# Neighbourhood attention: where a projection rests between its chunks, the order of the transfers, and the last head's output

## The chip, the core and the metric

One core of a Trainium2 chip runs the whole program in one launch. TensorE (PE) multiplies; VectorE (DVE), ScalarE (ACT) and GpSimd (POOL) work on its results; SyncE (SP) issues nearly all DMA transfers. Each engine runs its own list in order and waits on semaphores. The metric is the time of one execution in microseconds. It is 2857.19 us before the change, the median of three runs.

## The reference

The program is a trunk of two layers in fp32: a gated short convolution with its FFN, then neighbourhood attention with its FFN, and a final norm. Only the attention, its two projections and the passage into its output projection are touched.

```python
# layer 1 of a two-layer trunk; layer 0 is a gated short convolution, each layer ends in a SwiGLU FFN
def neighbourhood_attention(hl, hc, w_qkv, rpb, w_o, want_ctx):
    ...
    qkv = hl @ w_qkv                                   # 1024 latent tokens, 16 heads of 64
    kv_c = hc @ w_qkv[:, D:]                           # 256 context tokens: keys and values only
    ...
    def row_block(r):                                  # a row of 64 tokens of the 16 x 64 grid
        ...
        s_win = einsum('bhqd,bhrqcd->bhqrc', q_r, k_win) * scale + bias     # 8 x 16 window
        s_ctx = einsum('bhqd,bkhd->bhqk', q_r, k_ctx) * scale
        s = jnp.concatenate([s_win, s_ctx], axis=-1)
        p = jax.nn.softmax(s, axis=-1)
        ...
        return p_win @ v_win + p_ctx @ v_ctx
    ...
    yl = o.transpose(1, 0, 3, 2, 4).reshape(B, S, D) @ w_o
xl = xl + g1 * yl
```

## The kernel before

**Precision.** Every matrix product runs as three products of a high and a low part (`hi*hi`, `lo*hi`, `hi*lo`). So each intermediate is copied out of a PSUM bank twice: ScalarE writes the high part, and VectorE or GpSimd subtracts it for the low part.

**Pairs, units, groups.** The 16 heads make 8 pairs. For each pair the 1024 queries of each head are cut in four units of two blocks of 128, so a pair has 8 units, 0 to 3 for the first head and 4 to 7 for the second. A block scores against itself, its neighbours and the 256 context tokens: 640 keys, 512 at the ends. The turned probabilities of a unit are handled in three groups (`GROUPS`), so a pair has 24 slots: slot 3u + g is group g of unit u.

**TensorE's order.** In `attention` each slot does at most four things: `scores` of a block two units ahead (in groups 0 and 1 only), `fill` (a chunk of the Q or K projection of the NEXT pair), `turn` (transposes, two groups ahead), and `values` (the product with V). `values` of a unit's first group waits for `sum_done`, since all units share one PSUM bank. `QK_CHUNKS` says how many of a tile's 24 matmuls each slot gets. There are five tiles (`QK_TILES`): 0 is the context keys (256 columns), 1 and 3 are keys, 2 and 4 queries (512 columns); tiles 1 to 4 are those of the next pair, tile 0 that of the pair after. All use one bank, so behind each tile there is an empty slot, in which `QK_DRAINED` lets ScalarE (`qk_high`) and VectorE (`qk_low`) copy it out.

**ScalarE's order.** In a unit it takes `exponentials` of the next unit's first block, `pt_high` of group 0, the second `exponentials`, `pt_high` of group 1, `half` (the copy of half of the former unit's values), `pt_high` of group 2, and `out_high` (the high copy of the former unit's output). A drain stands behind its group's `pt_high`. `PANEL_AT` adds the high part of a weight panel at the end of two units. VectorE sums the halves (`head_sum`, which sets `sum_done`), GpSimd normalises the probabilities and makes low parts.

**SyncE's order.** Q and K go through DRAM: `store_qk` writes a tile, and `load_head0`, `load_late_keys0`, `load_late_queries0` and `load_head1` bring them back per head. A load waits until the store in front has landed, and all that is behind it on SP waits too. Unit outputs go from `o_st_hi` and `o_st_lo` to `o_dram` (`store_o`), and `load_o` brings them to `o_hi` and `o_lo` for the output projection, which multiplies eight blocks; block 7 is the last pair's.

**The ends.** Before the loop the first pair's five tiles are made in whole (`FIRST_BANKS`), among the last two tiles of V. The last pair has no projection to fill with.

## Time and profile before

| | |
|---|---|
| runs | 2856.08, 2857.23, 2857.19 us; median 2857.19 |
| profiled execution | 2855.52 us, its span 2853.7 us |
| PE busy | 2750.7 us, 96% |
| DVE, POOL, ACT busy | 1936.4, 1092.6, 952.6 us |
| attention | about 1588 to 2033 us of the span |
| output projection | about 2033 to 2137 us |

A row of a timeline has the start, the duration, the engine, the line and the operation with its tiles (out<-in); in square brackets stands how long the engine had been idle, and what released it. TensorE's records overlap, since a matmul's duration reaches to its last result: the pace is the difference between two starts. In rows of stretches PEclk is the granted clock of TensorE, 1.00 at 2.4 GHz and 0.50 at 1.2 GHz.

### The profile page before, as it was taken

Reading aid. Unit: us, or ns where it says so; the run is one execution under the profiler, and the core shown is the slowest. Engines: PE = TensorE matmul, PEld = TensorE weight load, DVE = VectorE, ACT = ScalarE, POOL = GpSimd, SP = SyncE. Lnnn points to the kernel's source line nnn. Section 1 sums busy time; section 2 is a strip of 40 time slices with the busy share of each in tenths; the row PEclk is TensorE's granted clock in tenths of the full one; section 3 lists DMA queues with packets and bytes.
Section 4 is the critical chain, followed back from the end, with each engine's and each line's share of the span. In section 5 each row is a group of like instructions: output and inputs, shape, how many; then the busy total and the mean of one; then the engine's idle time right before and its main releaser. Section 6 shows DMA issues by size and latency. Waiting matters only on the chain.

```text
span 2853.7 us, 42028 instructions
## 1 busy us (share of the span) xinstructions
PE 2750.7 (96%) x14290; PEld 2282.9 (80%) x14290; DVE 1936.4 (68%) x2826; ACT 952.6 (33%) x1678; POOL 1092.6 (38%) x792
## 2 busy tenths in 40 slices
PE   6999999999999999999999999999899999999998
PEld 3888888677788888889988788888777778888885
DVE  4677676778777777754765355656557877777777
ACT  4211111522222222244631466666423222222223
POOL 1212111125665565510011355445312566556552
PEclk9999999999999999999999999999999999999999
DMA  6421221032111111178567556555821011111111
GB/s 246 126 67 60 94 70 45 1 108 67 65 48 51 59 44 51 52 249 275 170 194 193 168 180 198 160 179 177 286 97 44 30 59 45 51 59 44 51 59 67
DMA packets 190148, 305.97 MB, mean 107 GB/s; under 512 B 58976, under 2 KB 123744, under 8 KB 190048
## 3 DMA queue, kind: packets, MB, share of 16 engines
q1 hardware_dynamic: 190048, 304.64, 33.1%
q8 instruction: 63, 1.03, 0.2%
q14 instruction: 37, 0.30, 0.0%
HBM read 255.28 MB, written 52.82 MB: 108 GB/s over the span
## 4 chain that ended last, share of the span: by engine, by line
PE 83%; DVE 5%; ACT 3%; DMA 3%; issue 3%; SPq 2%; POOL 1%; ACTq 0%; DVEq 0%; POOLq 0%
PE psum L1294 22%; PE psum L1146 20%; PE psum L1105 17%; PE psum L1479 6%; PE psum L1432 3%; PE psum L1344 3%; PE psum L1132 2%; PE psum L1538 2%; PE psum L1509 2%; PE psum L1355 1%; PE psum L1523 1%; DMA raw<-ffn_panels 1%; ACT probs L2025 1%; DVE w_lo L2387 1%; DVE residual L2250 1%
## 5 line engine op out<-in xcount | busy, mean ns | idle before, releaser
L2250 DVE SCALAR_TENSOR_TENSOR residual<-psum,modulation,residual 128x512 f32<-128x512 f32 x896 | 639.4, 729 | 376.2 <-PE psum L1146 372.8
L2791 POOL TENSOR_TENSOR w_lo<-raw,w_hi 128x1024 fp32r<-128x1024 f32 x118 | 295.5, 2511 | 909.0 <-ACT w_hi L1666 904.2
L1146 PE MATMUL psum<-prod_hi,w_hi 128*128 128x512 f32 x896 | 350.0, 391 | 11.3 <-DVE residual L2250 6.4
L1146 PE MATMUL psum<-prod_hi,w_lo 128*128 128x512 f32 x896 | 343.0, 383 | 0.0
L1146 PE MATMUL psum<-prod_lo,w_hi 128*128 128x512 f32 x896 | 343.0, 383 | 0.0
L2824 POOL TENSOR_TENSOR w_lo<-raw,w_hi 128x512 fp32r<-128x512 f32 x175 | 259.2, 1481 | 209.7 <-ACT w_hi L1829 209.7
L1666 ACT ACTIVATE w_hi<-raw 128x1024 fp32r<-128x1024 f32 x186 | 194.0, 1057 | 418.5 <-PE psum L1105 202.4
L1294 PE MATMUL psum<-act_hi,w_hi 128*128 128x512 f32 x700 | 273.6, 391 | 6.0 <-POOL w_lo L2824 5.9
L1294 PE MATMUL psum<-act_hi,w_lo 128*128 128x512 f32 x700 | 272.7, 390 | 0.0
L1294 PE MATMUL psum<-act_lo,w_hi 128*128 128x512 f32 x700 | 272.4, 389 | 0.0
L1146 PEld LDWEIGHTS psum<-prod_hi,w_hi 128*128 128x128 f32 x896 | 168.1, 188 | 70.8 <-DVE residual L2250 30.3
L1829 ACT ACTIVATE w_hi<-raw 128x512 fp32r<-128x512 f32 x175 | 109.4, 626 | 344.8 <-PE psum L1294 343.6
L1105 PE MATMUL psum<-act_hi,w_hi 128*128 128x512 f32 x728 | 194.8, 367 | 4.7 <-POOL w_lo L2809 3.0
L1146 PEld LDWEIGHTS psum<-prod_hi,w_lo 128*128 128x128 f32 x896 | 168.3, 188 | 34.0
L1105 PE MATMUL psum<-act_lo,w_hi 128*128 128x512 f32 x728 | 194.1, 366 | 0.0
L1105 PE MATMUL psum<-act_hi,w_lo 128*128 128x512 f32 x728 | 193.9, 366 | 0.0
L1146 PEld LDWEIGHTS psum<-prod_lo,w_hi 128*128 128x128 f32 x896 | 168.4, 188 | 28.3
L2462 DVE TENSOR_TENSOR part<-psum,part 128x512 f32<-128x512 f32 x245 | 167.3, 683 | 33.7 <-ACT part L1884 31.2
L2674 DVE TENSOR_TENSOR pt_lo<-psum,pt_hi 128x512 fp32r<-128x512 f32 (+1 forms) x192 | 111.0, 579 | 99.0 <-ACT pt_hi L2031 98.5
L1294 PEld LDWEIGHTS psum<-act_hi,w_hi 128*128 128x128 f32 x700 | 131.4, 188 | 36.0 <-POOL w_lo L2824 8.6
L1105 PEld LDWEIGHTS psum<-act_hi,w_hi 128*128 128x128 f32 x728 | 130.6, 188 | 32.5 <-ACT gate L1810 3.8
L1294 PEld LDWEIGHTS psum<-act_hi,w_lo 128*128 128x128 f32 x700 | 131.4, 188 | 28.0
(262 smaller groups left out, 6161.5 us busy)
## 6 DMA issues: line engine op xcount, KB each, us to landing
raw<-ffn_panels SPq DMA_DIRECT2D x198, 512.0 KB, 3.3
raw<-conv_panels SPq DMA_DIRECT2D x32, 512.0 KB, 5.4
rest_in<-mod_rest SPq DMA_DIRECT2D x40, 384.0 KB, 4.6
more_row<-mod_panels SPq DMA_DIRECT2D x48, 256.0 KB, 2.7
v_st<-v_dram SPq DMA_DIRECT2D x32, 320.0 KB, 4.9
mod_in<-mod_rest SPq DMA_DIRECT2D x24, 384.0 KB, 6.0
mod_early<-mod_panels SPq DMA_DIRECT2D x16, 512.0 KB, 15.2
raw<-qk_panels SPq DMA_DIRECT2D x16, 512.0 KB, 5.7
```

The costliest lines, as they stand in the source:

```text
L1105: mm = pe.matmul(psum[:, bank + b, 0:tn], w[:, s, kb, :], acts[h][:, kb, t0:t0 + tn], start=(kb == 0 and n == 0), stop=(kb == KB - 1 and n ...
L1146: mm = pe.matmul(psum[:, 6 + r % 2 if bank is None else bank, 0:tn], w[:, s, ob, :], h[:, t0:t0 + tn], start=(n == 0), stop=(n == 2))
L1294: mm = pe.matmul(psum[:, SEVEN_BANKS[n], :], w[:, where // 2, (where % 2) * KQ + q, :], moving[b][q], start=first, stop=last)
L1344: mm = pe.matmul(psum[:, bank, 0:TC], w[:, s, kb, :], h[:, kb, CTX], start=(kb == 0 and n == 0), stop=(kb == KB - 1 and n == 2))
L1479: mm = pe.matmul(psum[:, bank, 0:tn], w[:, s, kb, :], h[:, kb, t0:t0 + tn], start=(r == 0), stop=(r == QK_MATMULS - 1))
L1666: act.activation(panel(w_hi, s), raw[:, s], ACT.Copy).then_inc(hi_done[s], 1)
L1829: act.activation(quad(w_hi, where), source, ACT.Copy).then_inc(block_hi, 1)
L2250: dve.scalar_tensor_tensor(out=residual[:, ob, t0:t0 + tn], in0=psum[:, 6 + r % 2 if bank is None else bank, 0:tn], scalar=modulation[:, g ...
L2462: dve.tensor_tensor(part[:, out, :], psum[:, SEVEN_BANKS[n], :], part[:, other, :], ALU.add).then_inc(partial_dve, 1)
L2674: dve.tensor_tensor(pt_lo[:, at:at + n], psum[:, 4 + (group0[u] + g) % 2, 0:n], pt_hi[:, at:at + n], ALU.subtract).then_inc(pt_lo_done, 1)
L2791: pool.tensor_tensor(panel(w_lo, s), raw[:, s], panel(w_hi, s), ALU.subtract).then_inc(lo_done[s], 1)
L2824: pool.tensor_tensor(quad(w_lo, where), source, quad(w_hi, where), ALU.subtract).then_inc(block_lo, 1)
```

## The change

It does five things.

- `QK_CHUNKS`, `QK_DRAINED`: tile 1 takes slots 0 to 4 (5, 5, 5, 5, 4 matmuls), tile 2 slots 6 and 7 (12, 12), tile 3 slots 9 to 13, tile 4 slots 15 to 19, the narrow tile slots 21 and 22 (12, 12). The empty slots are 5, 8, 14, 20 and 23, where they were 4, 8, 13, 17 and 23. `PANEL_AT` moves one panel from unit 4 to unit 5.
- The first pair: all five tiles are made and drained first, the last two tiles of V after them, then the scores of two units. ScalarE's table load for the exponentials comes before the V copies.
- SP: in the first pair the late keys and queries go ahead of the V transfers; `load_head1` is split in keys and queries; in the loop the transfers stand in another order.
- The last pair's outputs are written to `o_hi` and `o_lo` in place, by rows of the head and not of two staging halves; the last stores and loads fall away. `head_sum` there waits for one unit later (`others` is 0).
- `last_pair` on TensorE waits for the low copies, not for a load.

TensorE, end of unit 6 in the loop (slots 19 or 20 and on; L1523 `turn`, L1538 `values`, L1509 `scores`, L1479 or L1478 the projection). Before, from the last matmul of the chunk in slot 20:

```order
L1479 MATMUL psum<-act_hi,w_lo 128x256
...
L1523 MATMUL psum<-ident,probs 128x128 [waits pt_lo_done]
L1538 MATMUL psum<-pt_hi,v_st 128x256 [waits pt_lo_done]
L1538 MATMUL psum<-pt_lo,v_st 128x256
L1538 MATMUL psum<-pt_hi,v_st 128x256
L1538 MATMUL psum<-pt_lo,v_st 128x256
...
L1509 MATMUL psum<-k_hi,q_st 128x256 [waits s_done]
L1509 MATMUL psum<-k_lo,q_st 128x256
L1509 MATMUL psum<-k_hi,q_st 128x384
L1509 MATMUL psum<-k_lo,q_st 128x384
```

After, from the last `values` of slot 19:

```order
L1538 MATMUL psum<-pt_lo,v_st 128x128
...
L1523 MATMUL psum<-ident,probs 128x128 [waits pt_lo_done]
L1538 MATMUL psum<-pt_hi,v_st 128x256 [waits pt_lo_done]
L1538 MATMUL psum<-pt_lo,v_st 128x256
L1538 MATMUL psum<-pt_hi,v_st 128x256
L1538 MATMUL psum<-pt_lo,v_st 128x256
...
L1509 MATMUL psum<-k_hi,q_st 128x256 [waits s_done]
L1509 MATMUL psum<-k_lo,q_st 128x256
L1509 MATMUL psum<-k_hi,q_st 128x384
L1509 MATMUL psum<-k_lo,q_st 128x384
...
L1478 MATMUL psum<-act_hi,w_hi 128x256 [waits lo_done1]
```

The chunk between the two `values` is gone: slot 20 is empty, and slot 21 starts a tile.

ScalarE, same place (`stage_hi` is a drain, `o_st_hi` the output copy, `w_hi` the panel, `probs` exponentials, `pt_hi` turned probabilities). Before:

```order
L2037 ACTIVATE o_half<-psum 64x256 [waits sum_done,pv_ready]
...
L2031 ACTIVATE pt_hi<-psum 128x512 [waits pt_ready]
L2044 ACTIVATE o_st_hi<-o_sum 64x256 [waits o_out1,sum_done]
L1666 ACTIVATE w_hi<-raw 128x1024 [waits raw_in0]
...
L2025 ACTIVATE probs,stats<-neg_s,stats 128x512 [waits s_done]
...
L2031 ACTIVATE pt_hi<-psum 128x512 [waits pt_ready]
...
L2025 ACTIVATE probs,stats<-neg_s,stats 128x640 [waits s_done]
```

After:

```order
L2035 ACTIVATE o_half<-psum 64x256 [waits sum_done,pv_ready]
...
L2029 ACTIVATE pt_hi<-psum 128x512 [waits pt_ready]
...
L2006 ACTIVATE stage_hi<-psum 128x512 [waits qk_out]
L2043 ACTIVATE o_st_hi<-o_sum 64x256 [waits o_out1,sum_done]
L1663 ACTIVATE w_hi<-raw 128x1024 [waits raw_in0]
...
L2023 ACTIVATE probs,stats<-neg_s,stats 128x512 [waits s_done]
...
L2029 ACTIVATE pt_hi<-psum 128x512 [waits pt_ready]
...
L2023 ACTIVATE probs,stats<-neg_s,stats 128x640 [waits s_done]
```

The drain of 512 columns now stands in front of the output copy, the panel and the next unit's exponentials.

SP, the first pair (`v_dram` stores of V, `k_dram` and `q_dram` stores of tiles 3 and 4). Before:

```order
L776 DMA v_dram<-stage_v_lo 128x8x64
L776 DMA v_dram<-late_v_hi 128x8x64 [waits v_lo_done,v_hi_done]
L776 DMA v_dram<-stage_v_lo 128x8x64
L799 DMA k_dram<-stage_hi 128x512 [waits qk_lo_done]
L799 DMA k_dram<-stage_lo 128x512
L813 DMA k_hi<-k_dram 64x512 [waits qk_out]
L813 DMA k_hi<-k_dram 64x512
L813 DMA k_lo<-k_dram 64x512 x2
L841 DMA v_st<-v_dram 128x640 x2
L799 DMA q_dram<-stage_hi 128x512 [waits qk_lo_done,v_out1,v_out0]
L799 DMA q_dram<-stage_lo 128x512
L807 DMA q_st<-q_dram 64x512 [waits qk_out]
```

After:

```order
L812 DMA k_dram<-stage_hi 128x512 [waits qk_lo_done]
L812 DMA k_dram<-stage_lo 128x512
L826 DMA k_hi<-k_dram 64x512 [waits qk_out]
L826 DMA k_hi<-k_dram 64x512
L826 DMA k_lo<-k_dram 64x512 x2
L812 DMA q_dram<-stage_hi 128x512 [waits qk_lo_done]
L812 DMA q_dram<-stage_lo 128x512
L820 DMA q_st<-q_dram 64x512 [waits qk_out]
L820 DMA q_st<-q_dram 64x512
L857 DMA v_st<-v_dram 128x640 [waits rest_summed]
L857 DMA v_st<-v_dram 128x640
L789 DMA v_dram<-late_v_hi 128x8x64 [waits v_lo_done,v_hi_done]
```

The stores of V went from in front of both tiles to behind them.

```diff
+        def staged_rows(i, u):
+            h0 = DH * (u // 4 if isinstance(i, int) and i == PAIRS - 1 else u % 2)
+            return slice(h0, h0 + DH)
+        def staged(i, u):
+            rows = staged_rows(i, u)
+            if isinstance(i, int) and i == PAIRS - 1:
+                q0 = 2 * P * (u % 4)
+                return rows, o_hi[rows, i, q0:q0 + 2 * P], o_lo[rows, i, q0:q0 + 2 * P]
+            return rows, o_st_hi[rows, :].bitcast(F32R), o_st_lo[rows, :].bitcast(F32R)
         def value_bank(i, u):
...
         QK_MATMULS = 3 * KB
-        FIRST_BANKS = (2, 3, 4, 5, PV_BANK)
+        FIRST_BANKS = (2, 3, 4, 5, 1)
...
-        QK_CHUNKS = {**chunks(1, 1, 0, (6, 6, 6, 6)), **chunks(1, 2, 5, (8, 8, 8)), **chunks(1, 3, 9, (6, 6, 6, 6)),
-                     **chunks(1, 4, 14, (8, 8, 8)), **chunks(2, 0, 18, (5, 5, 5, 5, 4))}
-        QK_DRAINED = {4: (1, 1), 8: (1, 2), 13: (1, 3), 17: (1, 4), 23: (2, 0)}
-        PANEL_AT = {4: 1, 6: 0}
+        QK_CHUNKS = {**chunks(1, 1, 0, (5, 5, 5, 5, 4)), **chunks(1, 2, 6, (12, 12)), **chunks(1, 3, 9, (5, 5, 5, 5, 4)),
+                     **chunks(1, 4, 15, (5, 5, 5, 5, 4)), **chunks(2, 0, 21, (12, 12))}
+        QK_DRAINED = {5: (1, 1), 8: (1, 2), 14: (1, 3), 20: (1, 4), 23: (2, 0)}
+        PANEL_AT = {5: 1, 6: 0}
...
-            def load_head1(i):
-                sp.wait_ge(qk_out, 32 * (NQK * i + Q_LAST + 1))
+            def load_keys1(i):
+                sp.wait_ge(qk_out, 32 * (NQK * i + K_LAST + 1))
                 at_least(sp, s_ready, 16 * i)
                 load_keys(i, 1, 0, T, head_in[1])
+            def load_queries1(i):
+                sp.wait_ge(qk_out, 32 * (NQK * i + Q_LAST + 1))
                 load_queries(i, 1, 0, TL, head_in[1])
...
             load_head0(0)
+            store_qk(0, K_LAST)
+            load_late_keys0(0)
+            store_qk(0, Q_LAST)
+            load_late_queries0(0)
             sp.wait_ge(rest_summed, MORE_GROUPS + V_LAST)
+            load_v(0, 0)
             store_v(V_LATE)
             store_v(V_LATE + 1)
-            store_qk(0, K_LAST)
-            load_late_keys0(0)
-            load_v(0, 0)
             for n in range(V_STAGES):
                 sp.wait_ge(v_out[n], 32 * len(V_ORDER) // V_STAGES)
-            store_qk(0, Q_LAST)
-            load_late_queries0(0)
-            load_head1(0)
+            load_keys1(0)
+            load_queries1(0)
             store_qk(1, 0)
...
                 first = isinstance(i, int) and i == 0
-                if panels:
-                    load_qk_panel(i + 2, 0)
-                    load_qk_panel(i + 2, 1)
-                elif heads:
-                    for s in range(2):
-                        load_panel("wo", s, 0, wo_panels[s])
-                load_v(i, 1)
+                if heads:
+                    load_bias(i + 1, 0)
                 if not first:
                     store_o(i - 1, UNITS - 1)
+                load_v(i, 1)
                 if not heads:
-                    load_o(2)
-                if heads:
-                    load_bias(i + 1, 0)
-                store_o(i, 0)
...
-                if not heads:
+                    for pair in range(2, PAIRS - 1):
+                        load_o(pair)
                     sp.wait_ge(s_ready, 2 * UNITS * PAIRS)
...
                         load_panel("wo", s, 0, wo_panels[s])
+                    return
+                store_o(i, 0)
+                store_qk(i + 1, 1)
+                for s in range(2):
+                    if panels:
+                        load_qk_panel(i + 2, s)
+                    else:
+                        load_panel("wo", s, 0, wo_panels[s])
+                store_o(i, 1)
+                store_qk(i + 1, 2)
+                load_head0(i + 1)
+                store_o(i, 2)
+                load_bias(i + 1, 1)
+                store_o(i, 3)
+                store_qk(i + 1, K_LAST)
+                load_v(i + 1, 0)
+                load_late_keys0(i + 1)
+                store_o(i, 4)
+                load_keys1(i + 1)
+                store_o(i, 5)
+                store_qk(i + 1, Q_LAST)
+                load_late_queries0(i + 1)
                 store_o(i, 6)
...
                     store_qk(i + 2, 0)
-                elif heads:
+                load_queries1(i + 1)
+                if not panels:
+                    load_o(0)
                     load_o(1)
...
-            for n in range(K_LAST):
+            for n in range(NQK):
                 if FIRST_BANKS[n] == V_REST_BANK:
                     pe.wait_ge(rest_ready, 2 * MORE_GROUPS + V_LAST)
+                if n == Q_LAST:
+                    pe.wait_ge(v_lo_done, V_LATE + 2)
                 qk_matmuls(0, n, FIRST_BANKS[n], 0, QK_MATMULS)
...
             v_tile(V_LATE + 1)
-            qk_matmuls(0, K_LAST, FIRST_BANKS[K_LAST], 0, QK_MATMULS)
...
                         values(i, u, g)
-            pe.wait_ge(v_lo_done, len(V_ORDER) + 4)
-            pe.wait_ge(qk_lo_done, K_LAST)
+            pe.wait_ge(qk_lo_done, NQK)
             for ab in range(2):
                 scores(0, 0, ab)
-            qk_matmuls(0, Q_LAST, FIRST_BANKS[Q_LAST], 0, QK_MATMULS)
-            scores(0, 1, 0)
+            for ab in range(2):
+                scores(0, 1, ab)
+            pe.wait_ge(v_lo_done, len(V_ORDER) + 4)
             qk_matmuls(1, 0, QK_BANK, 0, QK_MATMULS)
             pe.wait_ge(attn_consts, 5)
-            pe.wait_ge(qk_lo_done, K_LAST + 1)
             turn(0, 0, 0)
             turn(0, 0, 1)
-            scores(0, 1, 1)
-            pe.wait_ge(qk_lo_done, NQK)
             attention(0, 2)
...
                 if kb == PAIRS - 2:
-                    pe.wait_ge(o_last_in, 32)
+                    pe.wait_ge(o_lo_done, UNITS * PAIRS)
...
-                h0 = DH * (u % 2)
+                rows, high, _ = staged(i, u)
                 act.wait_ge(sum_done, UNITS * i + u + 1)
-                at_least(act, o_out[u % 2], 16 * UNITS * i + 32 * (u // 2))
-                act.activation(o_st_hi[h0:h0 + DH, :].bitcast(F32R), o_sum[h0:h0 + DH, :],
-                               ACT.Copy).then_inc(o_hi_done, 1)
+                if not (isinstance(i, int) and i == PAIRS - 1):
+                    at_least(act, o_out[u % 2], 16 * UNITS * i + 32 * (u // 2))
+                act.activation(high, o_sum[rows, :], ACT.Copy).then_inc(o_hi_done, 1)
...
                 n = UNITS * i + u
-                h0 = DH * (u % 2)
+                others = 0 if isinstance(i, int) and i == PAIRS - 1 else 1
                 dve.wait_ge(half_done, n + 1)
-                at_least(dve, o_hi_done, n - 1)
-                at_least(dve, o_lo_done, n - 1)
-                dve.tensor_tensor(o_sum[h0:h0 + DH, :], psum[0:DH, value_bank(i, u), 0:2 * P], o_half[0:DH, :],
+                at_least(dve, o_hi_done, n - others)
+                at_least(dve, o_lo_done, n - others)
+                dve.tensor_tensor(o_sum[staged_rows(i, u), :], psum[0:DH, value_bank(i, u), 0:2 * P], o_half[0:DH, :],
                                   ALU.add).then_inc(sum_done, 1)
```

## Rows read from the trace of the kernel before

**Rows 1.** The page's part 1: busy us (share of the span) of each engine.

```profile
PE 2750.7 (96%) x14290; PEld 2282.9 (80%) x14290; DVE 1936.4 (68%) x2826; ACT 952.6 (33%) x1678; POOL 1092.6 (38%) x792
```

**Rows 2.** Waits of PE, 1600 to 2120 us: line, releaser, total us, times, longest us.

```profile
PE psum L1538 <- DVE o_sum L2684: 10.9, 22, 0.6
```

**Rows 3.** Timeline of PE, first pair: start us, us, line, operation, [idle before, releaser].

```profile
1605.26 0.55 PE L1509 MATMUL psum<-k_hi,q_st 128*128 128x256 f32 x1 [5.83 <-issue]
...
1609.39 0.36 PE L1538 MATMUL psum<-pt_hi,v_st 128*128 128x256 f32 x1
```

**Rows 4.** Stretches: us, busy (instructions) of PE, PEld, DVE, ACT, POOL; PEclk; DMA share; GB/s.

```profile
1605.00:1609.00 4.00, 3.74 (x10) 3.11 (x11) 0.89 (x3) 0.00 (x0) 1.21 (x2) 0.50 0.99 251
1664.00:1719.60 55.60, 53.69 (x351) 47.77 (x349) 32.96 (x86) 34.65 (x80) 26.92 (x31) 1.00 0.57 176
1941.90:1995.00 53.10, 50.10 (x321) 43.61 (x319) 32.31 (x85) 34.35 (x79) 27.23 (x31) 1.00 0.58 179
2010.50:2027.30 16.80, 14.88 (x108) 12.86 (x106) 13.94 (x39) 15.14 (x37) 9.00 (x12) 0.96 0.85 288
```

**Rows 5.** Timeline of the DMA issues on SP, first pair.

```profile
1582.97 1.24 SPq L807 DMA_DIRECT2D q_st<-q_dram  x2
...
1601.90 1.11 SPq L807 DMA_DIRECT2D q_st<-q_dram  x2
```

**Rows 6.** Timeline of ACT, then DVE, first pair.

```profile
1601.96 0.38 ACT L2009 ACTIVATE stage_hi<-psum 128x256 fp32r<-128x256 f32 x1 [5.54 <-DMA q_dram<-stage_lo]
...
1590.18 0.82 DVE L2663 CUSTOM_DVE_ANT_0 neg_s<-psum,table 128x640 f32<-128x640 f32 x1
```

**Rows 7.** Timeline of PE, second pair, end of the sixth unit and after.

```profile
1704.55 0.60 PE L1523 MATMUL psum<-ident,probs 128*128 128x128 f32 x4
...
1706.58 0.28 PE L1479 MATMUL psum<-act_hi,w_hi 128*128 128x256 f32 x1
...
1707.81 0.66 PE L1523 MATMUL psum<-ident,probs 128*128 128x128 f32 x4 [0.47 <-DVE pt_lo L2674]
1709.03 0.39 PE L1538 MATMUL psum<-pt_hi,v_st 128*128 128x256 f32 x1 [0.56 <-DVE o_sum L2684]
```

**Rows 8.** Timeline of ACT, then DVE, same place.

```profile
1704.83 0.60 ACT L2009 ACTIVATE stage_hi<-psum 128x512 fp32r<-128x512 f32 x1 [2.29 <-PE psum L1479]
...
1708.02 0.38 ACT L2037 ACTIVATE o_half<-psum 64x256 f32<-64x256 f32 x1
...
1709.56 1.06 ACT L1666 ACTIVATE w_hi<-raw 128x1024 fp32r<-128x1024 f32 x1
...
1708.55 0.42 DVE L2684 TENSOR_TENSOR o_sum<-psum,o_half 64x256 f32<-64x256 f32 x1
```

**Rows 9.** Timeline of PE, third pair: its start, and its fourth unit.

```profile
1717.84 0.39 PE L1479 MATMUL psum<-act_hi,w_hi 128*128 128x512 f32 x1
...
1719.23 0.60 PE L1523 MATMUL psum<-ident,probs 128*128 128x128 f32 x4
1720.34 0.38 PE L1538 MATMUL psum<-pt_hi,v_st 128*128 128x256 f32 x1 [0.51 <-DVE o_sum L2684]
...
1742.61 0.38 PE L1538 MATMUL psum<-pt_hi,v_st 128*128 128x256 f32 x1 [0.45 <-DVE o_sum L2684]
```

**Rows 10.** Timeline of SP, second pair; issues 1704 to 1716 us (KB, us to landing).

```profile
1708.12 0.39 SPq L799 DMA_DIRECT2D q_dram<-stage_hi  x1
...
1710.90 1.19 SPq L807 DMA_DIRECT2D q_st<-q_dram  x2
...
q_st<-q_dram SPq DMA_DIRECT2D x2, 128.0 KB, 2.7
```

**Rows 11.** Timeline of ACT, last pair.

```profile
2005.61 0.42 ACT L2044 ACTIVATE o_st_hi<-o_sum 64x256 fp32r<-64x256 f32 x1 [5.18 <-DMA o_dram<-o_st_lo]
...
2010.10 0.41 ACT L2044 ACTIVATE o_st_hi<-o_sum 64x256 fp32r<-64x256 f32 x1 [0.49 <-DMA o_dram<-o_st_lo]
```

**Rows 12.** Timeline of PE, first product of the output projection.

```profile
2044.05 0.74 PE L1105 MATMUL psum<-o_hi,w_hi 128*128 128x512 f32 x2 [1.04 <-DMA o_lo<-o_dram]
```

More of the change, by code:

```diff
@@ L950, in _ @@
             load_residual(1)
-            store_o(PAIRS - 1, UNITS - 1)
-            for side in o_out:
-                sp.wait_ge(side, 16 * UNITS * PAIRS)
-            for dst, dram in zip((o_hi, o_lo), o_dram):
-                sp.dma_start(dst[:, PAIRS - 1].bitcast(F32), dram[PAIRS - 1]).then_inc(o_last_in, 16)
             for kb in range(2, KB):
@@ L2645, in _ @@
                     dve.memset(table[:, first:first + TC], 0.0).then_inc(attn_consts, 1)
+            for n in range(K_LAST, NQK):
+                qk_low(0, n, FIRST_BANKS[n])
             v_low(V_LATE)
             v_low(V_LATE + 1)
-            qk_low(0, K_LAST, FIRST_BANKS[K_LAST])
             dve.wait_ge(attn_consts, 5)
@@ L2938, in out_low @@
             def out_low(i, u, started):
-                h0 = DH * (u % 2)
-                if h0:
+                rows, high, low = staged(i, u)
+                if rows.start:
                     pool.wait_ge(probs_done, started)
                 pool.wait_ge(o_hi_done, UNITS * i + u + 1)
-                pool.tensor_tensor(o_st_lo[h0:h0 + DH, :].bitcast(F32R), o_sum[h0:h0 + DH, :],
-                                   o_st_hi[h0:h0 + DH, :], ALU.subtract).then_inc(o_lo_done, 1)
-                if h0:
+                pool.tensor_tensor(low, o_sum[rows, :], high.bitcast(F32), ALU.subtract).then_inc(o_lo_done, 1)
+                if rows.start:
                     pool.wait_ge(o_lo_done, UNITS * i + u + 1)
```

49 lines of the change are left out of this document (8 added, 41 removed).

## The prediction

> **What bounds the kernel now.** I read the page's busy shares first: TensorE is busy 96% of the span [rows 1], so only time that it stands idle, or runs at half clock, can be won. Then its waits in the attention stage: 10.9 us in 22 short waits for `o_sum` on VectorE, each 0.6 us or less [rows 2]. The timelines show where. (a) Before the third unit of the first pair TensorE idles 5.83 us until 1605.26 [rows 3]; the queries of that unit were issued only at 1601.90 [rows 5], since their store had waited behind everything else. It then runs at half clock, 0.50 from 1605 to 1609 [rows 4]. (b) In the steady pairs, 55.6 us each, it is 1.9 us idle by the records [rows 4]. Matmul records overlap, so I count from start to start, which gives 2.9. Three short losses return in every pair, each at `values` of a unit's first group, and each right after an EMPTY group that stood third in the unit before: slots 8, 17 and 23. The empty slots 4 and 13, second in their units, cost nothing. (c) In the last pair ScalarE waits 5.18 and 0.49 us for output stores [rows 11], and everything behind it stands. (d) In the output projection TensorE waits 1.04 us for the last output's way through memory [rows 12].
>
> **Step 1, the start.** What goes: 5.83 us, and half of the 3.8 us (1605.26 to about 1609.0) at half clock, 1.9: 7.7 us. The same matmuls are issued, only in another order, so TensorE reaches the first scores with nothing lost. But `Q_LAST`'s 24 matmuls (0.23 us each, by six from 1717.84 to 1719.23 [rows 9]; 5.5 us) no longer stand between the first scores and their softmax. The second unit's scores need the banks that VectorE empties at 0.7 to 0.82 us an operation [rows 6]: I count 1.2 us of new wait. The 24 narrow ones of the next pair (0.12 each, 2.9 us) cover exponentials and normalising. The third turn then waits for the first `pt_lo`, some 0.4 us, as ScalarE and VectorE are one drain behind. Net 7.7 - 1.6 = 6.1 won. Is a transfer late next? SP has issued the first head's loads by 1584.2 [rows 5]; then store K, load K, store Q, load Q follow. A store needs 2.8 us from issue to the load behind it [rows 10], or 5.5 as the nearest slow one [rows 6]; loads of keys take 2.5 us to issue, those of queries 1.2 and 2.7 to land [rows 10]. The queries land between 1596 and 1602, and are wanted near 1600.5; the values behind them up to 3 us late. So step 1 is worth 3 to 7.7 us; I take 6.1, as the store of [rows 10] is the same transfer in lighter traffic, and the heavy one had the values' loads around it.
>
> **Step 2, the steady pairs.** Take the place at slot 17 [rows 7, 8]. The last projection matmul of the tile is issued at 1704.55. ScalarE has been waiting for it 2.29 us, since its drain stands in front of the next unit's exponentials; it runs the drain at 1704.83, then the output copy, two exponentials, two copies of turned probabilities, and the half copy at 1708.02. VectorE's sum at 1708.55 releases `values` at 1709.03: 4.48 us after 1704.55. TensorE's own work on that way is turn, values, the empty group's turn and values, scores (2.03 us, up to 1706.58), the fill F, and a turn of 0.35. The loss is 4.48 - 2.38 - F. For slot 18, F = 5 x 0.12 = 0.6: 1.5 by this, 1.44 by the starts (1707.18 to 1707.81, 1708.22 to 1709.03). Slot 0 has F = 1.39: 0.75 lost (transposes at 1719.23, 0.35 of them, `values` at 1720.34 [rows 9]). Slot 9, also 1.39, loses 0.69 (idle 0.45 by its record where slot 0 has 0.51 [rows 9]). Fill plus loss is 2.04 to 2.14 at all three. That is the rule of this kernel: after an empty third group the next fill must be 2.1 us, or the difference is lost.
> The change makes ALL five empty groups third ones (5, 8, 14, 20, 23):
> - slot 6 has F = 12 x 0.23 = 2.77: nothing lost.
> - slot 9: five matmuls, 1.16; loss 0.92 (was 0.69).
> - slot 15: 1.16; two long exponentials, 4.1 against 4.0 us: loss 1.04 (new).
> - slot 21: F = 12 x 0.12 = 1.43, but in this unit ScalarE also splits the weight panel (`PANEL_AT` 6), which now stands between drain and exponentials: 1.06 long, 0.97 of its time (the copy at 1709.56 [rows 8]); 0.11 less for a narrow copy. 2.1 + 0.97 - 0.11 - 1.43 = 1.53 (slot 18 was 1.44).
> - slot 0: 2.13 - 1.16 = 0.98 (was 0.75).
> Sum 4.47 against 2.88: 1.59 us more per pair, 9.5 in the six pairs that project ahead. Slots 4 and 13 gave nothing to win back. If ScalarE had more slack than this, the cost would be 0; if the split were to delay GpSimd's normalising too, 2.5 us a pair, 15 in all. I take 9.5, as three places of the trace agree to 0.1.
>
> **Step 3, the seventh pair.** It has no narrow tile to fill with. The rows hold 3.0 us idle in 53.1 [rows 4], 4.7 by the starts. After it: 0.92 + 1.04, then slot 21 with F = 0 behind drain and split, 2.96, and the last pair's third-unit scores wait for queries that now leave one unit later, with nothing to cover it: 2.2. Together 7.1, so 2.4 more (bounds 0 and 4).
>
> **Step 4, the last pair.** Its outputs go straight to `o_hi`/`o_lo`, so ScalarE's 5.18 + 0.49 us go: 5.7. ScalarE is busy 15.1 of 16.8 us there [rows 4], so what it loses the span loses, and nothing else is late next: `o_sum` now has one buffer in place of two, but the previous low copy ends some 2 us before the next sum wants it. Bounds 3 and 6.
>
> **Step 5, the output projection.** 1.04 us idle, 1.2 by starts, go [rows 12]. The Trainium skill, page "DMA: Bandwidth & Descriptors", section "Anatomy of one DMA — SWDGE (gpsimd) path", puts a fixed 2 us or so on each transfer, most of it the receipt of the write. By it a store and a load back would be worth 4 us, and the sum 2.8 us lower. The row disagrees: the projection's first six blocks hide all but 1.2, and I go by the row.
>
> **Sum.** -6.1 + 9.5 + 2.4 - 5.7 - 1.2 = -1.1 us. From the profiled execution's 2855.52 that is 2854.4; the median of the runs stands 1.67 above that execution, so 2856.1, forecast 2856.0. This measurement tells apart about 0.2%, 5.7 us: no change to be seen.
>
> **Rivals.**
> - A, the forecast: 0.55; own range 2852 to 2861.
> - B, the third groups cost nothing more: for it, that slots 4 and 13 are free; against it, the three places above. Then steps 2 and 3 are 0 to 1: 2857.2 - 13 + 0.5 = 2844.7. Chance 0.20.
> - C, slower by late queries. `Q_LAST` is drained at slot 20, not 17. From the last projection matmul to the second query load's landing the trace has 9.65 us (1704.55; issue at about 1711.5, 2.7 to land [rows 7, 10]); TensorE now wants them after 9.1: 5.3 to the `values` of slot 21 (4.48 + 0.97 - 0.11), and 3.8 of its own work from there to the next pair's first group. The 0.5 of wait is hidden, because in the same step `values` waits anyway, until 12.2 against 11.8. From 0.5 us later on it costs the span in each of seven pairs. With the slow store of [rows 6], 2.7 us later, it is 2.2 x 7 = 15: 2871. For it, that the long key loads stand closer before; against it, quiet queues at that place. Chance 0.13.
> - D, a transfer takes the place of the wait at the start, and the last pair finds another: steps 1 and 4 at their low ends, -3 - 3 - 1.2 + 11.9 = +4.7: 2862. Chance 0.12.
> The clock is a part of this. The gaps of 5.83 and of about 5 us were followed by the 1.2 GHz level, those up to 1.5 us were not; the one of 3 us in step 3 lies between. If it counts, half a stretch like the first is lost, up to 1.9 us, inside A's range. The Trainium skill, page "TensorE: Matmul & The Clock Gate", section "Part 1: The HAM clock gate (the "warmup" mystery)", says that only an engine left idle falls to the lower level; by it the 1.5 us losses leave the clock alone, which the 1.00 of the steady pair bears out [rows 4].
> Faster by over 0.2%: B and a tail of A, 0.24. Slower: C, half of D and a tail of A, 0.21. Within: 0.55. The range goes from near B to half way to C: 2846 to 2866.
>
> **What would show it.** Right: no idle before 1610 over 1.5 us and no half clock there; pairs of 57.2 us in place of 55.6, with losses at slots 9, 15, 21 and 0; ScalarE without a DMA wait in the last pair; no wait at the projection's seventh block. Wrong: pairs of 55.6 us or less (B), TensorE waiting over 1 us before the third unit's scores in the steady pairs (C), a wait for `v_st` near 1603 (D).

## The result, and the profile after

The changed kernel is slower: 2867.11 us, median of seven runs (2864.01 to 2868.70), against 2856.37 for the kernel before in the same session (seven runs, 2855.01 to 2858.31). The ratio is 1.0035, 95% interval [1.0023, 1.0046]: 10 to 11 us more, where I had forecast no change at 2856.0 and a range up to 2866. The profiled execution took 2864.55 us, 9.0 more than that of before. TensorE runs the same 14290 matmuls, is busy 6.5 us longer by its records, and waits more; beside [rows 1]:

```profile
PE 2757.2 (96%) x14290; PEld 2282.0 (80%) x14290; DVE 1934.8 (68%) x2826; ACT 954.1 (33%) x1678; POOL 1093.0 (38%) x792
```

One execution of the kernel with the order undone, further below, took 7190.83 us and counts neither in its median nor in its ratio.

The two traces can be laid side by side at the same instructions. The first fence is the kernel before, the second the changed one (timeline of PE: start us, duration). The rows are `values` of the fourth unit in the first and in the seventh pair, the first product of the output projection, and the first product after the norm.

```profile
1631.56 0.39 PE L1538 MATMUL psum<-pt_hi,v_st 128*128 128x256 f32 x1 [0.42 <-DVE o_sum L2684]
...
1964.78 0.39 PE L1538 MATMUL psum<-pt_hi,v_st 128*128 128x256 f32 x1 [0.42 <-DVE o_sum L2684]
...
2033.22 0.47 PE L1105 MATMUL psum<-o_hi,w_hi 128*128 128x512 f32 x1 [0.97 <-issue]
...
2140.59 0.50 PE L1132 MATMUL psum<-act_hi,w_hi 128*128 128x512 f32 x1 [2.08 <-DVE act_lo L2224]
```

```profile
1627.99 0.39 PE L1538 MATMUL psum<-pt_hi,v_st 128*128 128x256 f32 x1 [0.45 <-DVE o_sum L2680]
...
1973.49 0.39 PE L1538 MATMUL psum<-pt_hi,v_st 128*128 128x256 f32 x1 [0.45 <-DVE o_sum L2680]
...
2041.35 0.70 PE L1104 MATMUL psum<-o_hi,w_hi 128*128 128x512 f32 x2 [0.97 <-issue]
...
2149.54 0.50 PE L1131 MATMUL psum<-act_hi,w_hi 128*128 128x512 f32 x1 [2.08 <-DVE act_lo L2219]
```

By differences of these starts:

| stretch | before | after | change | forecast |
|---|---|---|---|---|
| up to the first row (step 1) | | | -3.6 | -6.1 |
| six steady pairs (step 2) | 333.2 | 345.5 | +12.3 | +9.5 |
| seventh and last pair (steps 3, 4) | 68.4 | 67.9 | -0.6 | -3.3 |
| projection and norm (step 5) | 107.4 | 108.2 | +0.8 | -1.2 |

The 9.0 us are all in these four. Each stretch came out 2.0 to 2.8 us worse than forecast, all with the same sign. But 0.7 of the first 3.6 us lie ahead of anything that was changed: the last product of `prod_hi` and `w_hi` in the FFN ahead of the attention layer starts at 1452.54 before and at 1451.82 after. So the new start itself is worth 2.9. Where they went:

**The start.** The idle 5.83 us of [rows 3] are gone, and so is the half clock of [rows 4]; the row of the same stretch reads

```profile
1605.00:1609.00 4.00, 4.00 (x27) 3.56 (x26) 2.25 (x6) 2.17 (x5) 1.60 (x2) 1.00 0.90 213
```

But two waits are new. PE, ACT and SP of the changed kernel, in this order:

```profile
1614.41 0.39 PE L1509 MATMUL psum<-k_hi,q_st 128*128 128x256 f32 x1 [1.27 <-DMA q_st<-q_dram]
...
1616.41 0.49 PE L1478 MATMUL psum<-act_hi,w_hi 128*128 128x512 f32 x1 [1.26 <-DVE stage_lo L2631]
...
1615.03 0.60 ACT L2006 ACTIVATE stage_hi<-psum 128x512 fp32r<-128x512 f32 x1 [4.69 <-DMA k_dram<-stage_lo]
...
1600.49 0.74 SPq L789 DMA_DIRECT2D v_dram<-stage_v_lo  x1
1604.10 1.11 SPq L826 DMA_DIRECT2D k_hi<-k_dram  x2
...
1606.53 1.23 SPq L820 DMA_DIRECT2D q_st<-q_dram  x2
1607.81 0.58 SPq L812 DMA_DIRECT2D k_dram<-stage_hi  x1
```

SP waits from 1601.2 to 1604.1 for V's stores. Behind that wait stand head 1's keys and queries, for which TensorE waits, and the store of the next pair's context keys, for which ScalarE waits 4.69 us with its next drain. That is one of the two halves of rival D, a transfer in the place of the old wait, and it came at about D's price: D had this step at -3, the traces have -2.9.

**The steady pairs.** One of the first two pairs of the changed kernel, and a later one (columns of [rows 4]):

```profile
1711.80:1769.70 57.90, 54.18 (x350) 47.48 (x349) 33.15 (x85) 34.82 (x80) 26.89 (x31) 1.00 0.60 174
...
1827.20:1884.70 57.50, 54.45 (x350) 47.53 (x349) 33.14 (x85) 34.81 (x80) 26.93 (x31) 1.00 0.59 172
```

57.5 to 57.9 us where the forecast said 57.2 and [rows 4] had 55.6. I take the waits of PE from 1640 to 1960 us as the common measure, since that is nearly all steady pairs (5.8 of them before, 5.6 after). Before, then after (line, releaser, us in total, times, longest):

```profile
PE psum L1538 <- DVE o_sum L2684: 8.5, 17, 0.6
PE psum L1523 <- DVE pt_lo L2674: 2.7, 6, 0.5
```

```profile
PE psum L1538 <- DVE o_sum L2680: 8.2, 17, 0.6
PE psum L1523 <- DVE pt_lo L2670: 6.1, 12, 0.8
PE psum L1509 <- DMA q_st<-q_dram: 3.2, 4, 1.3
PE psum L1509 <- DVE stats L2659: 1.1, 2, 0.6
```

The waits at the turn doubled: they stand at slots 15 and 21 now, where before there was one in a pair, at slot 18. New is the wait for the late queries. Start to start, the losses at slots 9, 15 and 21 are 0.92, 1.25 and 1.61 us (forecast 0.92, 1.04, 1.53), and then 1.4 and 1.3 us for the queries in the first two pairs, 0.5 to 0.8 later, where slot 0 was to lose 0.98.

**The seventh and the last pair.** ScalarE has no wait for a transfer left in the last pair, so the 5.7 us of [rows 11] are gone. But at the boundary TensorE waits longer than step 3 allowed, and the clock falls, as it had not before (1.00 from 1983 to 1998 there). PE, then the window:

```profile
2000.36 1.11 PE L1523 MATMUL psum<-ident,probs 128*128 128x128 f32 x4 [2.10 <-DVE pt_lo L2670]
...
2007.53 0.58 PE L1509 MATMUL psum<-k_hi,q_st 128*128 128x256 f32 x1 [2.56 <-DMA q_st<-q_dram]
```

```profile
1998.00:2012.00 14.00, 9.34 (x50) 8.26 (x49) 7.76 (x21) 8.80 (x22) 9.05 (x10) 0.76 0.76 203
```

At the next pair of like rows, in the last pair, before and after, the two steps can be told apart:

```profile
2001.07 0.63 PE L1523 MATMUL psum<-ident,probs 128*128 128x128 f32 x4 [0.49 <-POOL probs L2935]
...
2015.17 0.63 PE L1523 MATMUL psum<-ident,probs 128*128 128x128 f32 x4 [0.45 <-POOL probs L2930]
```

Counted from the seventh pair's fourth unit, that is 36.3 us before and 41.7 after: +5.4 for step 3, where +2.4 was forecast. From there to the projection it is 32.2 and 26.2: -6.0 for step 4, forecast -5.7.

**Projection and norm.** The wait of [rows 12] is gone. Afterwards TensorE is at the 1.2 GHz level longer: over the 14 us that end 2.5 us ahead of the last row above, before and after,

```profile
2124.05:2138.05 14.00, 9.85 (x51) 5.53 (x49) 4.92 (x16) 3.36 (x7) 0.00 (x0) 0.88 0.01 2
```

```profile
2133.00:2147.00 14.00, 10.37 (x42) 5.82 (x42) 4.51 (x16) 3.36 (x7) 0.00 (x0) 0.63 0.01 2
```

The list of small matmuls there is the same, 51 of them stand in the one window and 42 in the other, and nothing in the change touches them; by the table the passage took 2.0 us more than the forecast. Two kernels below that share this code (the ends alone, the order undone) have a clock of 0.73 and 0.76 there. And two that have the kernel before's own code from the projection on (exponentials ahead, longer fills) took 110.8 and 109.7 us from the projection to this row, where before took 107.4. So the passage varies by up to 3.5 us with nothing changed in it. What sets it, no run shows.

### The profile page after: what moved, and what is told of

It reads as the page before. It is cut to its first block, busy times and chain, and to the rows that moved or that the text cites. A ratio compares the mean times of both kernels' runs of the same rounds, so it can differ in the third digit from the quotient of the medians.

```text
span 2862.8 us, 42000 instructions
## 1 busy us (share of the span) xinstructions
PE 2757.2 (96%) x14290; PEld 2282.0 (80%) x14290; DVE 1934.8 (68%) x2826; ACT 954.1 (33%) x1678; POOL 1093.0 (38%) x792
## 4 chain that ended last, share of the span: by engine, by line
PE 82%; DVE 5%; ACT 3%; DMA 3%; issue 3%; SPq 2%; POOL 1%; ACTq 0%; DVEq 0%; POOLq 0%
PE psum L1293 22%; PE psum L1145 20%; PE psum L1104 17%; PE psum L1478 5%; PE psum L1343 4%; PE psum L1431 3%; PE psum L1354 2%; PE psum L1131 2%; PE psum L1538 2%; PE psum L1509 2%; PE psum L1523 1%; ACT probs L2023 1%; DVE residual L2245 1%; DMA q_dram<-stage_lo 1%; SPq L616 1%
## 5 line engine op out<-in xcount | busy, mean ns | idle before, releaser
L1293 PEld LDWEIGHTS psum<-act_hi,w_hi 128*128 128x128 f32 x700 | 131.4, 188 | 36.3 <-POOL w_lo L2819 8.7
```

Of the source, the lines that this page charges most:

```text
L1293: mm = pe.matmul(psum[:, SEVEN_BANKS[n], :], w[:, where // 2, (where % 2) * KQ + q, :], moving[b][q], start=first, stop=last)
```

## The experiments

Each was timed in turn with the kernel before on the same chip; medians of 4 to 11 runs, and a ratio to before with its 95% interval. Profiles are of one execution each. Before had medians of 2857.4 to 2859.6 there.

### The slot tables alone

The kernel before with the three new tables, nothing else.

```diff
-        QK_CHUNKS = {**chunks(1, 1, 0, (6, 6, 6, 6)), ...
-        QK_DRAINED = {4: (1, 1), 8: (1, 2), 13: (1, 3), 17: (1, 4), 23: (2, 0)}
+        QK_CHUNKS = {**chunks(1, 1, 0, (5, 5, 5, 5, 4)), ...
+        QK_DRAINED = {5: (1, 1), 8: (1, 2), 14: (1, 3), 20: (1, 4), 23: (2, 0)}
...
-        PANEL_AT = {4: 1, 6: 0}
+        PANEL_AT = {5: 1, 6: 0}
```

> The kernel before with the new slot tables alone (QK_CHUNKS, QK_DRAINED, PANEL_AT); start, transfers and last pair as before. Theory 1, the five empty third groups cost the time: the losses of a steady pair go from 2.9 to 4.7 us (slots 9, 15, 21 and 0 at 0.9, 1.25, 1.6, 1.0), 10 to 11 us in six pairs, and 2 more in the seventh: 2867 to 2870. The late queries cost nothing here, since only four output stores stand before them: they land 2 us earlier than in the changed kernel. Theory 2, the new order of the transfers in the loop costs it: 2857, and the losses at slots 15 and 21 are absent.

2870.93 us, ratio 1.0047 [1.0034, 1.0061]: +11.3. The tables alone cost as much as the whole change. Waits, 1640 to 1960 us:

```profile
PE psum L1538 <- DVE o_sum L2684: 11.7, 23, 0.6
PE psum L1523 <- DVE pt_lo L2674: 6.1, 12, 0.8
```

23 waits in place of 17: four in a pair, not three. There is no wait for queries, and the pairs are 57.5 us long all the same.

### The tables of before in the changed kernel

The reverse: the changed kernel, with the old tables put back.

> The changed kernel with the slot tables of before; start, order of transfers and last pair stay changed. Theory 1: the steady pairs lose 2.9 us again and not 4.9, the seventh 2.4 less, so 2867 - 12 - 2 = 2853, and the gains of start (3.6) and last pair (about 5.7) show against the kernel before: 2847 to 2853. Some 0.5 us a pair may stay for late queries, whose store is still issued behind the sixth output store. Theory 2: 2865 or more.

2887.18 us, ratio 1.0101 [1.0085, 1.0116]. My expectation failed by 34 us, on the side of its rival.

```profile
PE psum L1509 <- DMA q_st<-q_dram: 19.4, 5, 4.3
PE psum L1538 <- DVE o_sum L2680: 5.6, 11, 0.6
PE psum L1523 <- DVE pt_lo L2670: 2.7, 6, 0.5
```

The losses at the empty groups went back to their old size, but SP's new order stores the queries only behind unit 5's output, and close behind head 1's keys: the store of the high part takes 4.7 to 5.1 us to land in each of the first five pairs, where it takes 2.1 to 2.7 in the changed kernel. The old tables also leave TensorE less work between that output and the point where it wants the queries; how the two share the wait was not tried apart. The order of the transfers is a second cost, and it is tied to the tables. So neither part can be undone by itself to read off the other.

### ScalarE: exponentials ahead of the drain

The kernel before; after slots 8 and 17 the first exponentials of the unit after next go ahead of the drain.

```diff
                     pt_high(i, u, 2)
+                    if ahead_of_drain(u):
+                        exponentials(i, u + 2, 0)
                     drain(group0[u] + 2)
```

> The kernel before; only ScalarE's order is changed: at the empty third groups 8 and 17 the first exponentials of the unit after next are issued ahead of the tile's drain, not behind it. Nothing else. Theory 1 says that ScalarE stands idle 2.3 us in front of the drain and that its work behind the drain sets the loss: 0.8 us of it moves into the idle time, the loss at slot 9 (0.69) goes and that at slot 18 (1.44) falls to 0.6, 1.5 us a pair, 10 in seven pairs: 2846 to 2848. If the loss is TensorE's own (the shared bank, the sum on VectorE), nothing changes: 2857.

2857.22 us, ratio 0.9993 [0.9984, 1.0002]: nothing, where I had expected 10 us. The timeline of ACT, then DVE, third pair, behind slot 17, says why:

```profile
1762.56 0.72 ACT L2025 ACTIVATE probs<-neg_s,stats 128x512 f32<-128x512 f32 x1 [0.58 <-DVE stats L2668]
...
1763.29 0.36 ACT L2031 ACTIVATE pt_hi<-psum 128x256 fp32r<-128x256 f32 x1
1763.67 0.38 ACT L2037 ACTIVATE o_half<-psum 64x256 f32<-64x256 f32 x1
...
1761.23 0.69 DVE L2641 SCALAR_TENSOR_TENSOR stage_lo<-psum,stage_hi 128x512 fp32r<-128x512 f32 x1 [2.19 <-ACT stage_hi L2009]
1761.84 0.68 DVE L2668 CUSTOM_DVE_ANT_0 neg_s<-psum,table 128x512 f32<-128x512 f32 x1
...
1764.20 0.42 DVE L2689 TENSOR_TENSOR o_sum<-psum,o_half 64x256 f32<-64x256 f32 x1
```

It is the SECOND exponentials that are late: they wait for `neg_s`, which stands behind `stage_lo` on VectorE, which waits for the drain. `half` stands behind them. The wait at the turn shrank from 0.63 to 0.24 us, and that at `values` grew from 0.81 to 1.08.

### Longer fills

The kernel before, with the same 24 matmuls of a tile dealt out as 9, 5, 5, 5 and 14, 4, 2, 2, 2, the long chunk behind the third empty group.

```diff
-        ... chunks(1, 3, 9, (6, 6, 6, 6)), ... chunks(2, 0, 18, (5, 5, 5, 5, 4))}
+        ... chunks(1, 3, 9, (9, 5, 5, 5)), ... chunks(2, 0, 18, (14, 4, 2, 2, 2))}
```

> The kernel before with longer chunks behind the empty third groups: tiles 1 and 3 in chunks of 9, 5, 5, 5 (before 6, 6, 6, 6), the narrow tile in 14, 4, 2, 2, 2 (before 5, 5, 5, 5, 4); the empty slots stay. By fill + loss = 2.1 us: slots 0 and 9 fill 2.08 and lose nothing, slot 18 fills 1.68 and loses 0.4. That is 2.5 us a pair, 15 in six pairs: 2842. Against it, the last units of a pair keep only 0.24 us of fill in three slots, and ScalarE needs 4.2 to 5.2 us a unit there: up to 1 us a pair may come back, 2842 to 2848. If the loss does not depend on the fill, 2857.

2846.83 us, ratio 0.9960 [0.9947, 0.9974]. A gain from a table of numbers alone.

```profile
PE psum L1538 <- DVE o_sum L2684: 2.7, 11, 0.4
```

### The ends alone

The changed kernel with the old tables AND the old order of transfers in the loop (the edits of "The tables of before in the changed kernel" and of "The order of transfers undone" together): the new start, last pair and read-back remain.

> The changed start, last pair and wo read-back, with the slot tables and SyncE's loop order of the kernel before. Theory (the loss is all in the loop, and the ends gain what the traces showed): start -3.6, last pair about -5.7, wo projection +0.9 (its longer half-clock stretch), sum -8.4, so about 2848.5 beside 2857 (2844 to 2852). Rival (the ends gain nothing of themselves, the new waits at the start eat them): 2856 to 2858.

2848.56 us, ratio 0.9968 [0.9957, 0.9980]: -8.9. The ends as a whole are a gain. The parts did not come as expected, though, by the profiled execution (2851.93 us, the highest of the six): the last pair wins 6.0 us, but the start, counted from the same FFN product as above, only 0.8 and not 3.6, since TensorE waits 3.57 us for `stage_lo` there. The old table starts tile 2 in slot 5 and not 6, and the store that the drain in front of it waits for is as late as in the changed kernel.

### The order of transfers undone

The changed kernel with only SP's loop order of before.

```diff
...
                 store_o(i, 4)
-                load_keys1(i + 1)
-                store_o(i, 5)
                 store_qk(i + 1, Q_LAST)
                 load_late_queries0(i + 1)
+                store_o(i, 5)
+                load_keys1(i + 1)
...
```

> The changed kernel with SyncE's loop order of before; its slot tables stay new. Ledger theory (tables +11.3, ends -8.4, so the order of transfers carries the other +7.8): 2860 beside 2857, 7 us under the changed kernel, and no wait of TensorE for the late queries. Rival (the late queries are late because tile 4 is drained only in slot 20, whatever the order): 2866 to 2869 and the same waits of 0.5 to 1.4 us.

2860.76 us, ratio 1.0010 [1.0001, 1.0019]. The waits, and SP in the second pair:

```profile
PE psum L1539 <- DVE o_sum L2681: 11.7, 23, 0.6
PE psum L1524 <- DVE pt_lo L2671: 6.1, 12, 0.8
```

```profile
1709.91 0.37 SPq L812 DMA_DIRECT2D q_dram<-stage_hi  x1
...
1712.67 1.19 SPq L820 DMA_DIRECT2D q_st<-q_dram  x2
```

In the changed kernel the same two rows are

```profile
1712.24 0.38 SPq L812 DMA_DIRECT2D q_dram<-stage_hi  x1
...
1715.63 1.25 SPq L820 DMA_DIRECT2D q_st<-q_dram  x2
```

The wait for the queries is gone, and 17 waits for `o_sum` have become 23: the missing one at slot 0 is back. So in the later steady pairs the two are alternatives, and a pair is 57.5 us by either. The new order cost 0.4 us in each of the first two pairs and, from the seventh pair's fourth unit to the projection, 2.9. The profiled executions differ by 2.7 us, the ratios by about 7; what lies between I leave open. The parts nearly add: +11.3 for the tables and -8.9 for the ends make +2.4, and this kernel, which has both, stands at +3.4. So the loss is the tables', the ends take most of it back, and the order of the transfers adds 3 to 7 us.

### The ends with longer fills

The ends alone, and the edit of the longer fills on them.

> The ends alone (start, last pair, wo read-back changed; loop order of before) with the longer fills of nine and fourteen matmuls behind the two third empty groups. The two gains lie in different stages, so they should add: -8.4 and -12.8, about 2836 beside 2857 (2832 to 2841). Rival (they overlap, since a faster pair moves the waits for transfers): 2843 to 2848, no better than the long fills alone.

2838.00 us, ratio 0.9928 [0.9916, 0.9941]. Gains in different stretches add.

### One store earlier at the start

```diff
+            store_qk(1, 0)
             for n in range(V_STAGES):
                 sp.wait_ge(v_out[n], 32 * len(V_ORDER) // V_STAGES)
             load_keys1(0)
             load_queries1(0)
-            store_qk(1, 0)
```

> The changed kernel with the store of pair 1's first key tile issued ahead of SyncE's wait for the V stores. Theory: ScalarE's drain at the first pair's start no longer waits 4.7 us for that store, TensorE's 1.4 us wait ahead of the first pair's third fill goes, -1.4, so 2866 where the changed kernel stands at 2867 (the trace tells it, the times hardly). Rival: the wait is taken over by another one there, no gain.

2862.92 us, ratio 1.0019 [1.0010, 1.0027]. The wait for `stage_lo` is gone and that for the queries fell from 1.3 to 0.4 us (1590 to 1640 us):

```profile
PE psum L1509 <- DMA q_st<-q_dram: 0.4, 1, 0.4
```

Counted from that last FFN product, which starts at 1452.97 here, to `values` of the fourth unit at 1626.72, the start is worth 5.3 us beside before, where it is 2.9 in the changed kernel. So 2.4 us of what step 1 is short of its 6.1 were one store behind a wait it did not need. The profiled execution gained 2.5 us, the median some 4.

### The half copies ahead

The changed kernel; in the unit behind a drained third group `half` goes ahead of the second exponentials, and `head_sum` ahead of the second `pt_low`.

```diff
+                    early = not last and not (first and u == 0) and after_drain(u)
+                    if early:
+                        half(*before(i, u))
                     if more:
                         exponentials(nxt_i, nxt_u, 1)
                     pt_high(i, u, 1)
...
```

> The changed kernel with, in the unit after each drained third group (u = 0, 2, 3, 5, 7, but the last pair), the half copy ahead of the second exponentials on ScalarE, and head_sum ahead of the second pt_low on VectorE. Theory (what `values` waits for, 0.69 to 0.80 us at slots 9, 15 and 21, is the end of one chain: drain, neg_s, second exponentials, pt_high, half, o_sum; half needs nothing of the middle of it): these three waits fall to 0 to 0.2, 1.5 to 2 us a pair, about -11 in seven pairs, 2856 where the changed kernel stands at 2867; the waits at the turn (0.45, 0.92) stay. Rival (o_sum is late since VectorE itself is, stage_lo and neg_s ahead of it): less than 3 us in all.

2870.37 us, ratio 1.0040 [1.0026, 1.0054]: no gain, where I had expected 11 us. Yet the mechanism did what was expected of it, the waits for `o_sum` are all gone:

```profile
PE psum L1512 <- DMA q_st<-q_dram: 15.2, 6, 4.1
PE psum L1526 <- DVE pt_lo L2676: 6.1, 12, 0.8
```

The queries took all of it and more. TensorE now comes for them earlier; their store is issued later than with the old order, behind head 1's keys (four transfers of 320 KB), and the load that needs it stands 5.5 us behind it, where it is 3.4 in the changed kernel and 2.8 in [rows 10]:

```profile
1712.80 0.38 SPq L815 DMA_DIRECT2D q_dram<-stage_hi  x1
...
1718.33 1.19 SPq L823 DMA_DIRECT2D q_st<-q_dram  x2
```

The Trainium skill, page "DMA: Bandwidth & Descriptors", section "Latency and other measured facts", says that a transfer's fixed cost is small when the memory is lightly loaded and grows under load. The trace agrees in direction: the same 256 KB store lands in 2.7 us in the changed kernel and in 4.7 here, closer behind the keys, in the second pair; over the first four pairs it is 2.1 to 2.7 there and 2.7 to 4.7 here. It does not tell a slower memory from standing in line behind the keys' 1.3 MB.

### The same copies on the ends, with and without longer fills

Three kernels on the ends alone, with the earlier store of the start: with the longer fills; with fills and half copies ahead; with half copies ahead and the old fills.

> The ends with the longer fills and the loop order of before, and the store of pair 1's first key tile ahead of the wait for the V stores. Theory: the 3.8 us wait of TensorE for stage_lo at the first pair's slot 5 goes, at most 1 us of it comes back as another wait: 2834.5 to 2836 beside 2838 for the same kernel without the earlier store. Rival: late loads of head 1 land later behind that store and take it all back, 2838.

> The one before with the half copies ahead as well (units 0, 3 and 6). With long fills little is left to win: waits for o_sum of 0.34 and 0.45 us a pair. Theory: -0.8 a pair, -5, 2830. Rival (a half copy ahead of the second exponentials delays these, and the long fills had already covered the chain): no gain or a loss of 2.

> The same without the longer fills: ends, earlier store, half copies ahead, old fills of six and five matmuls. If the chain through half is what `fill + loss = 2.1` stood for, slots 9, 18 and 0 lose 0.6 to 0.7 us less each: 2848.5 - 3 (store) - 12 = 2833. Rival (VectorE late of itself, so the long fills remain the better cure): 2842 to 2846.

2834.29 (ratio 0.9917 [0.9904, 0.9931]), 2832.54 (0.9913 [0.9897, 0.9928]) and 2831.70 us (0.9909 [0.9894, 0.9924]). The last is the fastest here, 27 us under before, and needs no new table: its waits from 1640 to 1960 us, and one pair:

```profile
PE psum L1527 <- DVE pt_lo L2677: 2.7, 6, 0.5
```

```profile
1699.50:1753.00 53.50, 53.03 (x350) 47.58 (x349) 32.56 (x85) 34.76 (x80) 27.01 (x30) 1.00 0.62 186
```

17 waits for `o_sum` became none. So what step 2 called "fill plus loss is 2.1 us" is the length of one chain: drain, `stage_lo`, `neg_s`, second exponentials, `pt_high`, `half`, `o_sum`. `half` needs only the end of the former unit's `values`, and stands last by the order of the code. The Trainium skill, page "PSUM — Partial Sum Buffer", section "Engine vs sequencer instructions", says that the queues of ScalarE, VectorE and GpSimd are strictly first in, first out; these runs show what that costs, 0.7 to 0.8 us at each of three places in a pair. With fills and copies both (2832.54) nothing more comes of it, and the copies took only 1.75 us off the kernel with long fills, where I had expected 5: they are two cures for one wait.

### What makes the queries late

The half copies ahead, once with SP's whole loop order of before, once with only head 1's keys moved behind the late queries.

```diff
                 store_o(i, 4)
-                load_keys1(i + 1)
                 store_o(i, 5)
                 store_qk(i + 1, Q_LAST)
                 load_late_queries0(i + 1)
+                load_keys1(i + 1)
```

> The changed kernel with the half copies ahead and SyncE's loop order of before (new slot tables). Theory (the half copies won nothing on the changed kernel because the late queries, stored 2.3 us later than in the order of before and behind the long keys of head 1, became the last wait): with the old order TensorE no longer waits for them and the 2.7 us a pair of waits for o_sum go: 2861 - 15 = 2844 to 2847. Rival (the late queries are late because tile 4 is drained in slot 20, and become the last wait here too): 2854 to 2861.

> The changed kernel with the half copies ahead and only one entry moved in SyncE's order: the keys of head 1 behind the late queries (the store of the queries stays behind the fifth output store). Theory: the queries' store lands in 2.8 us instead of 5.5, TensorE's wait for them falls from 2.1 to under 1 us a pair: 2858 to 2862 where the same kernel with the keys ahead stands at 2870. Rival (the wait is for the fifth output store alone, the keys do no harm): 2868 to 2871.

2842.72 us (ratio 0.9942 [0.9928, 0.9955]) and 2855.30 (0.9989 [0.9980, 0.9998]), against 2870 with the keys ahead. Waits of the first, then of the second, 1640 to 1960 us:

```profile
PE psum L1527 <- DVE pt_lo L2677: 6.1, 12, 0.8
```

```profile
PE psum L1512 <- DMA q_st<-q_dram: 7.9, 6, 2.5
PE psum L1526 <- DVE pt_lo L2676: 5.9, 11, 0.8
```

The order makes them late, not the drain in slot 20. The keys' place is half of it (15.2 to 7.9 us of waits; 1.3 a pair where I had expected under 1, though the time came out better than expected). The rest goes with the other entries; that the fifth output store alone makes it was not tried apart. And the first of these kernels against the fastest above, 11.0 us, prices the new tables with the copies out of the way. A part of it is the earlier store at the start, which only the fastest has, worth 2.5 by its trace; the rest is the turn's waits, 12 against 6 of them, a pair of 54.8 us against 53.5, and the seventh pair's wait of 2.1.

## Why the prediction was wrong, step by step

**Step 1, the start: right in kind, twice too large.** The gap and its half clock went, the 1.2 and 0.4 us of new waits came about as worked out (1.18 and 0.31). The step stopped at the late queries and values, and did not follow SP's list to the store of the next pair's first tile. It was worth 2.9 us where I took 6.1, just under its low bound of 3 (the 3.6 of the table has 0.7 from ahead of the change). With that store moved, 2.4 us more came.

**Step 2, the steady pairs: the mechanism right, two sizes off.** The rule of 2.1 us stood up three ways: the tables alone, the longer fills, the half copies. Its losses were 4.6 us a pair against the 4.47 forecast, slot 15 being the mis-sized one: 1.25 for 1.04, as two waits, 0.45 at the turn and 0.80 at `values`. Start to start a pair grew by 1.9 us, not 1.59. The sentence that failed is "The 0.5 of wait is hidden, because in the same step `values` waits anyway". Later in the loop it holds; in the first two pairs the queries came 0.4 us too late for it.

**Step 3, the seventh pair: the step that failed most.** It measured +5.4 us, where I had taken +2.4 and bounded it at 4. The sum of its waits was right: TensorE's idle time over the stretch is 5.9 us after against 3.2 before. The term that failed is the clock, which I put at nothing in the sum and at 1.9 us at most in the range. The wait of 2.10 us at the turn (2.25 from start to start) and that of 2.56 for the queries (2.7, forecast 2.2) were each followed by the 1.2 GHz level, a clock of 0.76 over 14 us. That is 3.4 us of clock, about 3 of them on work: an estimate from these rows, and all that the step is short. The run with the old order of transfers has the wait at the turn alone and a clock of 0.88 there, and is 2.9 us shorter.

**Step 4, the last pair: right.** 6.0 us went, forecast 5.7, and nothing took the place of ScalarE's waits.

**Step 5: the term right, the stretch not.** The 1.2 us went; some 2 us of half clock in the norm passage took its place. This is the piece I can't explain by the change, and kernels with unchanged code there show as much (110.8 and 109.7 us for 107.4). Without it the time would have been near 2865, an estimate from the table: that this piece fell the wrong way was bad luck.

**The rivals.** B fell with the tables alone. C's mechanism, the late queries, is the one that was at work, at a quarter of its price in this kernel (0.4 twice and 2.9, of 15) and at its full price with the half copies ahead (2.1 us and more a pair). I had held "quiet queues at that place" against it, while the new order of SP has head 1's keys one output store ahead of the queries' store. D came true at the start (2.9 us, where it said 3) and not in the last pair. The deeper fault is in the sum: it took every step at its middle, and each new wait that it left out could only lengthen the time. Four stretches, four errors of 2 to 3 us, one sign, though the fourth was no wait.

## What to carry to other kernels

When a stall returns at regular places, write down the whole chain that ends it, across engines, and ask of each link whether it needs the link before or only stands behind it in a queue: moving one copy forward here was worth as much as the best table. Removing a wait is worth only the slack of the next one, so read how late each transfer is issued and what travels beside it before counting a gain. A table of slots and an order of transfers are one schedule; changing or undoing one without the other can cost more than either.

## What the runs showed of the hardware

In the second pair the same 256 KB store landed in 2.7 us in the changed kernel, in 4.7 closer behind head 1's keys, and in 2.1 with the keys moved behind it. And the clock: waits of 2.1 and 2.6 us at the seventh pair's end were followed by 0.76 over 14 us, the one of 2.1 alone by 0.88; with the half copies ahead, one of 4.1 us by 0.63 over 9 us, and the next, 2.0 us, by 0.84 over 11. But the length of a single wait does not decide it. With the keys later, a wait of 2.47 us until 1716.13 left the clock at 1.00 from 1713 to 1727. And in the ends alone waits of 0.98 and 0.6 us near 1986 were followed by 0.88 over 14 us, where the kernel before, with the same waits at the same place, kept 1.00. I had looked for a border between 1.5 and 5 us; these rows show none.
